# Gate rows by transfers in a two-half inference step, and another order of work between its halves

## The chip, the cores and the metric

One core of one Trainium2 chip runs one layer of a diffusion backbone for 384 tokens. The metric is the device time of one execution in microseconds (us), the median of three. A tile is given as partitions x columns. The engines are TensorE (PE), VectorE (DVE), ScalarE (ACT), GpSimd (POOL) and SyncE (SP), which issues most transfers.

## The reference, cut to what matters

```python
D_MODEL = 2048; SEQ = 128; DEC_SEQ = 256; FFN_HIDDEN = 5632      # 128 context and 256 latent tokens
def rmsnorm(x, g=None):
    y = x * rsqrt(mean(x * x, -1) + 1e-6)
    return y if g is None else y * g
# per layer, with mod = silu(cond) @ w_mod + b_mod, six vectors of 2048 for each of two conditions
# (c_ctx for context tokens, c for latent tokens): shift_m, scale_m, gate_m, shift_f, scale_f, gate_f
u  = (rmsnorm(x, g0) * (1 + scale_m) + shift_m) @ w_in            # 2048 x 5120
y1 = mixers(u) @ w_out                                           # attention and a scan; 2048 x 2048
x  = x + gate_m * rmsnorm(y1, g1)
h  = rmsnorm(x, g2) * (1 + scale_f) + shift_f
y2 = (silu(h @ w_gate) * (h @ w_up)) @ w_ffn_out                 # 2048 x 11264, 5632 x 2048
x  = x + gate_f * rmsnorm(y2, g3)
```

The last line but one of each half is where a gate comes in: one value for each of the 2048 columns, the same for all tokens of a condition.

## The kernel before

**Numbers and stages.** The 384 tokens are three blocks `tb` of 128 rows: block 0 is context, blocks 1 and 2 are latent. All matmuls are fp32 made of three rounded ones: a weight tile is split into `whi` (ScalarE, L468) and `wlo`, the remainder (VectorE, L1232); activations are split into `h_hi` and `h_lo` in the same way; TensorE adds hi x hi, lo x hi and hi x lo. Weights come as tiles of 1 MB in a fixed order, `PLAN`. The stages are: modulation and input projection (40 steps), output projection (16 steps), the work between the halves, FFN up (44 pairs of tiles), FFN down (4 groups `n` of 512 columns with 11 tiles `q` each, counted `v = 11 n + q`).

**Weight slots.** `tile_slots` gives each tile one of six slots of raw weights, the one that comes free first. SyncE issues each tile's transfer as soon as the slot's previous tile was used (`w_used`). The split is at most one tile ahead of TensorE: `whi` has room for two tiles, and `wlo` is written over the raw tile.

**Order.** Each engine's instructions are written out by hand. `gap(s, tb)` is what an engine does after block tb of step s: attention pieces, adds of a partial y1 (L1498) and, in the last four steps of the output projection, the row sums of y1 (ScalarE L644). The loops over s place splits (`lo`, `hi`) and gaps around each other.

**Gates.** The gate values lie as columns, one per partition, in `modc`. To multiply rows by them, every partition needs the whole row. `diagonal` (VectorE L1533) writes four 128x128 diagonal matrices of gate values into `diag` or `diag_b`; `gains` (TensorE L1114) multiplies a matrix of ones by them, so that a PSUM bank holds 512 gate values in every partition. There are 16 such calls: 8 in the last four steps of the output projection, two in each, and 8 in FFN down, after tiles q = 4 and 8 of each n. `y1_gate` (VectorE L1548) multiplies y1 by a bank, `y_gate` (L1542) does so for y2; the last group's banks are first copied to `gate_sb` on ScalarE (L777).

**Between the halves.** For each block VectorE does `residual(tb)`: gate the last 512 columns of y1, then four times x = x + y1 * scale over 512 columns (L1621). ScalarE squares x (L744) into `dump`, two halves per block, and sums them; GpSimd adds the two sums and takes the power -0.5 (L1886 to L1889); `norm_diagonal` (VectorE L1630) makes a diagonal of it; TensorE multiplies x by this diagonal (`x_transpose`, L960), which scales and transposes at once; VectorE applies scale and shift into `xnT` (L1304, L1306), ScalarE rounds to `h_hi` (L517), VectorE takes the remainder `h_lo` (L1311). The FFN's first tiles go k by k (k is one of 16 groups of 128 input rows), with six matmuls each (L1166 through `up_k`) and the transposes of k + 5 behind them. While TensorE waits it runs filler matmuls of 128 columns (L1155): 26, 10 and 5 ahead of the three blocks.

**End.** After the last tile VectorE gates the last columns and writes x in halves of 1024 columns (L1704); SyncE stores each half (L451).

## Time and profile before

| | us |
|---|---|
| median of three runs | 1792.37 |
| lowest, highest | 1792.31, 1792.74 |
| the profiled execution | 1791.8 |
| its span in the trace | 1790.0 |
| TensorE busy in it | 1761.8 |
| VectorE busy | 945.6 |
| ScalarE busy | 660.1 |
| GpSimd busy | 127.1 |

The span runs from the first to the last recorded instruction. A busy time is the union of an engine's instructions. The "chain that ended last" is followed back from the last instruction, at each step to whatever released it. One fp32 matmul from unsplit operands shows as two records. Matmuls are pipelined, so that the distance between starts, and not a record's length, is what one costs.

### The profile page before, as it was taken

The page shows a single profiled execution, that of the slowest core. Times are in us where ns is not written, and L with a number is a line of the kernel's source. Part 1 is how long each engine was busy: PE and PEld are TensorE (multiplying, and loading weights), DVE is VectorE, ACT ScalarE, POOL GpSimd, SP SyncE. Part 2 cuts the span into 40 slices and gives each one's busy share as a digit, 9 for nine tenths or more (in the row PEclk, how much of TensorE's full clock was granted, in tenths as well). Part 3 has the DMA queues.
Part 4 walks back from the last instruction along what each step waited for, and adds up shares of the span by engine and source line. Part 5 has one row for each costly group of instructions (what it writes and reads, how often), then busy time and mean ns, then how long its engine had stood idle before and what let it go on. Part 6 is the DMA issues. An engine that isn't in the chain of part 4 may idle for free.

```text
span 1790.0 us, 22643 instructions
## 1 busy us (share of the span) xinstructions
PE 1761.8 (98%) x9491; PEld 1524.9 (85%) x9491; DVE 945.6 (53%) x1276; ACT 660.1 (37%) x952; POOL 127.1 (7%) x179
## 2 busy tenths in 40 slices
PE   6999999999999999999999999999999999999998
PEld 4676666677778879999999999999999988888886
DVE  5465578633557677355665633333333455555554
ACT  3432354434564343222222222222222344444542
POOL 1001145410300010000000000000000000000000
PEclk9999999999999999999999999999999999999999
DMA  9998777765422333345545533333333333333321
GB/s 397 368 335 311 288 293 288 285 241 234 141 95 90 116 148 118 129 177 188 196 180 191 204 123 131 128 119 140 118 123 136 118 135 124 119 140 118 124 112 71
DMA packets 47190, 317.37 MB, mean 177 GB/s; under 512 B 5449, under 2 KB 7681, under 8 KB 10289
## 3 DMA queue, kind: packets, MB, share of 16 engines
q1 hardware_dynamic: 44736, 305.35, 45.5%
q0 software_dynamic: 2288, 10.56, 1.8%
q8 instruction: 75, 1.23, 0.3%
q14 instruction: 27, 0.21, 0.0%
q10 hardware_dynamic: 64, 0.02, 0.0%
HBM read 310.52 MB, written 5.39 MB: 176 GB/s over the span
## 4 chain that ended last, share of the span: by engine, by line
PE 96%; DVE 1%; DMA 1%; ACT 1%; POOL 0%; issue 0%; SPq 0%; DVEq 0%; POOLq 0%
PE ps L1166 41%; PE ps L943 8%; PE ps L945 8%; PE ps L944 8%; PE ps L837 7%; PE ps L838 7%; PE ps L836 7%; PE ps L815 4%; PE ps L1056 1%; PE ps L1079 1%; PE ps L1114 1%; PE ps L903 1%; PE ps L905 1%; PE ps L904 1%; PE ps L1006 1%; DMA xT<-in_x_t 0%
## 5 line engine op out<-in xcount | busy, mean ns | idle before, releaser
L1232 DVE TENSOR_TENSOR wlo<-raw,whi 128x1024 fp32r<-128x1024 f32 x376 | 459.0, 1233 | 687.2 <-ACT whi L468 687.1
L468 ACT ACTIVATE whi<-raw 128x1024 fp32r<-128x1024 f32 x376 | 392.3, 1058 | 831.4 <-PE ps L1166 507.0
L1166 PE MATMUL ps<-h_hi,whi 128*128 128x384 f32 x1408 | 471.4, 335 | 0.5 <-DVE h_lo L1311 0.5
L1166 PE MATMUL ps<-h_hi,wlo 128*128 128x384 f32 x1408 | 470.4, 334 | 0.0
L1166 PE MATMUL ps<-h_lo,whi 128*128 128x384 f32 x1408 | 470.3, 334 | 0.0
L1166 PEld LDWEIGHTS ps<-h_hi,whi 128*128 128x128 f32 x1408 | 264.3, 188 | 0.7 <-issue 0.7
L1166 PEld LDWEIGHTS ps<-h_lo,whi 128*128 128x128 f32 x1408 | 264.3, 188 | 0.0
L1166 PEld LDWEIGHTS ps<-h_hi,wlo 128*128 128x128 f32 x1408 | 264.3, 188 | 0.0
L943 PE MATMUL ps<-whi,h_hi 128*128 128x512 f32 x624 | 259.9, 417 | 0.0
L945 PE MATMUL ps<-wlo,h_hi 128*128 128x512 f32 x624 | 244.5, 392 | 0.0
L944 PE MATMUL ps<-whi,h_lo 128*128 128x512 f32 x624 | 243.6, 390 | 0.0
L836 PE MATMUL ps<-whi,j_hi 128*128 128x512 f32 x516 | 204.0, 395 | 0.0
L838 PE MATMUL ps<-wlo,j_hi 128*128 128x512 f32 x516 | 200.9, 389 | 0.0
L837 PE MATMUL ps<-whi,j_lo 128*128 128x512 f32 x516 | 200.9, 389 | 0.0
L943 PEld LDWEIGHTS ps<-whi,h_hi 128*128 128x128 f32 x624 | 117.2, 188 | 54.3 <-issue 30.3
L945 PEld LDWEIGHTS ps<-wlo,h_hi 128*128 128x128 f32 x624 | 117.1, 188 | 26.0
L944 PEld LDWEIGHTS ps<-whi,h_lo 128*128 128x128 f32 x624 | 117.5, 188 | 25.1 <-issue 1.9
L836 PEld LDWEIGHTS ps<-whi,j_hi 128*128 128x128 f32 x516 | 96.9, 188 | 21.8 <-issue 1.9
L837 PEld LDWEIGHTS ps<-whi,j_lo 128*128 128x128 f32 x516 | 96.8, 188 | 21.8 <-issue 1.9
L838 PEld LDWEIGHTS ps<-wlo,j_hi 128*128 128x128 f32 x516 | 96.8, 188 | 20.2
L1647 DVE TENSOR_TENSOR j_lo<-h3T,j_hi 128x1536 fp32r<-128x1536 f32 x44 | 77.4, 1758 | 8.4 <-ACT j_hi L771 8.4
L1869 POOL TENSOR_TENSOR smalls<-smalls 128x3 f32<-128x3 f32 x2 | 0.4, 190 | 1027.0 <-ACT ps L734 998.2
(257 smaller groups left out, 1362.1 us busy)
## 6 DMA issues: line engine op xcount, KB each, us to landing
raw<-in_weights SPq DMA_DIRECT2D x277, 1024.0 KB, 4.8
raw_x<-in_weights SPq DMA_DIRECT2D x6, 1024.0 KB, 19.5
xT<-in_x_t SPq DMA_DIRECT2D x4, 768.0 KB, 6.8
out<-x_sb SPq DMA_DIRECT2D x6, 512.0 KB, 2.7
x_sb<-in_x_sample POOLq DMA_DIRECT2D x1, 2048.0 KB, 12.2
sbc<-silu_rows POOLq DMA_DIRECT2D x1, 2048.0 KB, 8.1
raw<-in_weights SPq DMA_DIRECT2D x2, 512.0 KB, 18.4
gw<-in_lru_gate_w SPq DMA_DIRECT2D x4, 256.0 KB, 2.8
```

What stands on the lines that cost most here:

```text
L468: nc.scalar.activation(whi[:, 2 * (g % RING) + b], raw_of(t)[:, HK * b:HK * b + HK].rearrange("p k n -> p (k n)"), ACT.Copy).then_inc(w_hi, 1)
L815: ins = nc.tensor.matmul(ps[mod_bank(m)][32 * kk:32 * kk + 32, :], stat[:, 2 * k:2 * k + 32], raw_of(t)[:, kk, :], start=(kg == 0), stop=( ...
L836: nc.tensor.matmul(acc, xh[:, kk + HK * b, xs], wh[:, cols], start=(k == 0), stop=False)
L837: nc.tensor.matmul(acc, xl[:, kk + HK * b, xs], wh[:, cols], start=False, stop=False)
L838: ins = nc.tensor.matmul(acc, xh[:, kk + HK * b, xs], wl[:, cols], start=False, stop=(k == k_last))
L903: nc.tensor.matmul(acc, h_hi[:, k, xs], wh[:, cols], start=(k == 0), stop=False)
L943: nc.tensor.matmul(acc, h_hi[:, k, xs], wh[:, cols], start=begin, stop=False)
L944: nc.tensor.matmul(acc, h_lo[:, k, xs], wh[:, cols], start=False, stop=False)
L945: ins = nc.tensor.matmul(acc, h_hi[:, k, xs], wl[:, cols], start=False, stop=end)
L1166: return nc.tensor.matmul(ps[bank][:, 0:T], w[:, k % KH * P:(k % KH + 1) * P], xs[:, k, :], start=first, stop=last)
L1232: V.tensor_tensor(wlo[:, 2 * SLOT[t] + b], raw_of(t)[:, HK * b:HK * b + HK].rearrange("p k n -> p (k n)"), whi[:, 2 * (g % RING) + b].bitc ...
L1647: V.tensor_tensor(j_lo[v % 2][:, :, :], h3T[:, KG * q:KG * q + KG, :], j_hi[v % 2][:, :, :].bitcast(F32), ALU.subtract).then_inc(jl, 1)
```

## The change

**Gate rows.** `diagonal` and `gains` go, with all their calls, and `diag_b` and `gate_sb`. Gate columns are transposed instead: for each condition one matmul against the identity turns 16 columns of `modc` into a [16 x 128] tile; ScalarE copies both to `rows_g`; GpSimd stores them to DRAM (`gate_rows`) and reads them back with partition step 0, so that all 128 partitions hold the row of 2048. For the first gate this goes to `gate_r`, four pieces of 1024 columns laid over parts of `h_hi` and `h_lo` that the output projection has used up; the transposes stand at the end of the input projection, and the transfers wait for 12 adds of y1. For the second it goes to `gate2`, laid over weight slots 4 and 5. So tiles of FFN down may use four slots only. Its transposes stand behind down tile v = 1, the copy behind v = 3.

**Order between the halves.** In the last steps the gates of y1 stand ahead of the split of the next tile. After the last step the last add comes first, then the three residuals, then the diagonals. Block 2 is squared in four parts. Filler is 45, 0 and 2. For the first FFN tiles the four matmuls on `h_hi` stand ahead of the two on `h_lo`, each with a wait of its own.

**End.** The last block is stored in three parts: 1024, 512 and 512 columns.

The diff, cut to its core:

```diff
-        open_to = range(RAW + EXTRA) if key in early else range(RAW)
+        open_to = range(RAW + EXTRA) if key in early else range(RAW - 2 if key[0] == "down" else RAW)
...
+    gate_r = [[at(f"gate_r{c}{b}", [P, D // 2], H0 + off) for b, off in enumerate(offs)]
+              for c, offs in enumerate(((30720, 43008), (6144, 18432)))]
+    rows_g = at("rows_g", [KD, 2, P], P0 + 3072)
-    gate_sb = at("gate_sb", [P, 2, NC], U0 + 8192)
-    diag_b = at("diag_b", [P, KG, P], U0 + 43008)
+    gate2 = [at(f"gate2_{c}", [P, D], RW0 + (RAW - 2 + c) * KG * NC * 4) for c in range(2)]
...
+        def y_parts(tb):
+            ends = [0, D // 2, D] if tb < TB - 1 else [0, D // 2, D - NC, D]
+            return [slice(a, b) for a, b in zip(ends, ends[1:])]
+        def x1_parts(tb):
+            return 4 if tb == TB - 1 else 2
...
@@ ScalarE
                 if g == TB * IN_STEPS - 1:
                     act.wait_ge(st_t, 1)
+                    nc.scalar.activation(rows_g[:, :, :].rearrange("k c p -> k (c p)"), ps[3][0:KD, P:3 * P], ACT.Copy).then_inc(st_cp, 1)
...
-                for b in range(2):
+                w = D // x1_parts(tb)
+                for b in range(x1_parts(tb)):
                     act.wait_ge(x1_ok, 2 * tb + b + 1)
...
+                    if v == 3:
+                        act.wait_ge(gf_tr, 1)
+                        nc.scalar.activation(rows_g[:, :, :].rearrange("k c p -> k (c p)"), ps[7][0:KD, 0:2 * P], ACT.Copy).then_inc(gf_row, 1)
...
-            for j in range(2):
-                nc.scalar.activation(gate_sb[:, j, :], ps[7 - j][:, :], ACT.Copy).then_inc(gate_ok, 1)
@@ TensorE
-                nc.tensor.matmul(ps[gain_bank(idx)][:, :], ones[:, :], src[:, :, :].rearrange("p f n -> p (f n)"),
-                                 start=True, stop=True).then_inc(g_ps, 1)
...
+                    pe.wait_ge(gm_ok, 1)
+                    nc.tensor.transpose(ps[3][0:8, 0:P], stc[:, :], ident[:, :])
+                    for c in range(2):
+                        ins = nc.tensor.transpose(ps[3][0:KD, P + c * P:2 * P + c * P], modc[:, G_M:G_M + KD, c], ident[:, :])
...
-                if g >= TB * (STEPS - OUT_N) and g % TB < 2:
-                    gains(2 * (g // TB - STEPS + OUT_N) + g % TB)
...
-            for tb, busy in enumerate((26, 10, 5)):
+            for tb, busy in enumerate((45, 0, 2)):
...
+                pe.wait_ge(h_hs, KD + k + 1)
+                for part in range(2):
+                    b, wh, wl = now[part]
+                    up(k, part, wh, h_hi, k == 0, False)
+                    up(k, part, wl, h_hi, False, False)
                 pe.wait_ge(h_ls, KD + k + 1)
                 for part in range(2):
                     b, wh, wl = now[part]
-                    ins = up_k(k, part, wh, wl)
+                    ins = up(k, part, wh, h_lo, False, k == KD - 1)
...
-                    if q in (4, 8):
-                        gains(8 + 2 * n + q // 4 - 1)
+                    if v == 1:
+                        pe.wait_ge(gf_ok, 1)
+                        for c in range(2):
+                            ins = nc.tensor.transpose(ps[7][0:KD, c * P:P + c * P], modc[:, G_F:G_F + KD, c], ident[:, :])
@@ VectorE
-                                    ps[7 if tb == 0 else 6][:, :], ALU.mult).then_inc(y_g, 1)
+                                    gate2[1 if tb == 0 else 0][:, n * NC:(n + 1) * NC], ALU.mult).then_inc(y_g, 1)
...
-                if s:
-                    lo(*step_key(s + 1))
                 if n > 0:
                     for tb in range(TB):
                         y1_gate(n - 1, tb)
+                if s:
+                    lo(*step_key(s + 1))
...
+            gap(STEPS - 1, 2)
             residual(0)
-            gap(STEPS - 1, 2)
             residual(1)
+            residual(2)
             norm_diagonal(0)
-            residual(2)
             norm_diagonal(1)
@@ GpSimd
+            pool.dma_start(gate_d.rearrange("c (k p) -> k c p", p=P), rows_g[:, :, :]).then_inc(grow_w, 16)
...
+            pool.wait_ge(grow_w, 16)
+            pool.wait_ge(y_add, TB * OUT_N)
+            for c in range(2):
+                for b in range(2):
+                    pool.dma_start(gate_r[c][b][:, :], bass.AP(tensor=gate_d.tensor, offset=D * c + D // 2 * b,
+                                                               ap=[[0, P], [1, D // 2]])).then_inc(grow_in, 16)
...
+            pool.wait_ge(gf_row, 1)
+            pool.dma_start(gate2_d.rearrange("c (k p) -> k c p", p=P), rows_g[:, :, :]).then_inc(gf_w, 16)
+            pool.wait_ge(gf_w, 16)
+            pool.wait_ge(w_used, used(*LAST_UP))
+            for c in range(2):
+                pool.dma_start(gate2[c][:, :], bass.AP(tensor=gate2_d.tensor, offset=D * c, ap=[[0, P], [1, D]])).then_inc(gf_in, 16)
```

How it moves instructions, at two places. VectorE from the last adds of the output projection to the diagonals, before (`y_3` is y1's last group of 512 columns, `smalls` holds row scales):

```order
L1498 TENSOR_TENSOR y_3_120<-y_3_120,ps 128x512 [waits y_add,acc_ps] x2
L1548 TENSOR_TENSOR y_3_120<-y_3_120,ps 128x512 [waits y_sq,g_ps,x1_in]
L1621 SCALAR_TENSOR_TENSOR x_sb<-y_0_117,smalls,x_sb 128x512 [waits rs_done,y_g]
...
L1498 TENSOR_TENSOR y_3_120<-y_3_120,ps 128x512 [waits y_add,w_used]
L1548 TENSOR_TENSOR y_3_120<-y_3_120,ps 128x512 [waits y_sq,g_ps]
...
L1630 TENSOR_SCALAR diag<-par,smalls 128x128 [waits g_ps,rs_done]
L1548 TENSOR_TENSOR y_3_120<-y_3_120,ps 128x512 [waits y_sq,g_ps]
...
L1630 TENSOR_SCALAR diag<-par,smalls 128x128 [waits rs_done]
L1232 TENSOR_TENSOR wlo<-raw_86,whi 128x1024 [waits w_hi]
```

The same place in the changed kernel:

```order
L1507 TENSOR_TENSOR y_3_130<-y_3_130,ps 128x512 [waits y_add,acc_ps] x2
L1507 TENSOR_TENSOR y_3_130<-y_3_130,ps 128x512 [waits y_add,w_used,x1_in]
L1549 TENSOR_TENSOR y_3_130<-y_3_130,gate_r_114 128x512 [waits y_sq]
L1620 SCALAR_TENSOR_TENSOR x_sb<-y_0_127,smalls,x_sb 128x512 [waits rs_done,y_g]
...
L1549 TENSOR_TENSOR y_3_130<-y_3_130,gate_r_112 128x512 [waits y_sq]
...
L1549 TENSOR_TENSOR y_3_130<-y_3_130,gate_r_112 128x512 [waits y_sq]
...
L1629 TENSOR_SCALAR diag<-par,smalls 128x128 [waits grow_w,rs_done]
L1629 TENSOR_SCALAR diag<-par,smalls 128x128 [waits rs_done]
L1241 TENSOR_TENSOR wlo<-raw_86,whi 128x1024 [waits w_hi]
```

The last add moved ahead of the first gate and residual, and the first diagonal behind the third residual; the gates read `gate_r` and no PSUM bank.

TensorE after the output projection, before:

```order
L1155 MATMUL ps<-par,ones 128x128 x25
L960 MATMUL ps<-diag,x_sb 128x128 [waits xn_done,x1_ok,y_g]
...
L1155 MATMUL ps<-par,ones 128x128 x10
...
L1155 MATMUL ps<-par,ones 128x128 x5
L960 MATMUL ps<-diag,x_sb 128x128 [waits xn_done,x1_ok,y_g]
L960 MATMUL ps<-diag,x_sb 128x128 x8
L1166 MATMUL ps<-h_hi,whi 128x384 [waits h_ls,w_lo]
L1166 MATMUL ps<-h_lo,whi 128x384
```

In the changed kernel:

```order
L1156 MATMUL ps<-par,ones 128x128 x44
L977 MATMUL ps<-diag,x_sb 128x128 [waits xn_done,x1_ok,y_g]
...
L1156 MATMUL ps<-par,ones 128x128 x2
L977 MATMUL ps<-diag,x_sb 128x128 [waits xn_done,x1_ok,y_g]
L977 MATMUL ps<-diag,x_sb 128x128 x8
L1167 MATMUL ps<-h_hi,whi 128x384 [waits h_hs,w_lo]
L1167 MATMUL ps<-h_hi,wlo 128x384
L1167 MATMUL ps<-h_hi,whi 128x384
L1167 MATMUL ps<-h_hi,wlo 128x384
L1167 MATMUL ps<-h_lo,whi 128x384 [waits h_ls]
```

The filler moved ahead of block 0's transposes, and the first matmuls wait for `h_hs`, which counts columns of `h_hi`, and no longer for `h_ls`, which counts those of `h_lo`.

## Rows read from the trace of the kernel before

**Rows 1.** The page, chain that ended last: share of the span by engine.
```profile
PE 96%; DVE 1%; DMA 1%; ACT 1%; POOL 0%; issue 0%; SPq 0%; DVEq 0%; POOLq 0%
```

**Rows 2.** Chain in order of time: start us, us, engine, output, line, records.
```profile
494.82 0.48 PE ps L1096 x3
...
622.36 0.86 PE ps L1114 x2
...
632.33 0.86 PE ps L1114 x2
...
677.15 1.06 PE ps L1166 x6
...
678.88 1.06 PE ps L1166 x6
...
1672.74 0.86 PE ps L1114 x2
...
1730.77 0.86 PE ps L1114 x2
...
1764.32 0.86 PE ps L1114 x2
```

**Rows 3.** Lines L1498 and L1548: count, ns min/median/max, first and last start us.
```profile
L1498 DVE TENSOR_TENSOR y1p<-y1p,ps x3: 686/687/687, 571.4 to 578.1; 128x512 f32<-128x512 f32 x3
...
L1548 DVE TENSOR_TENSOR y<-y,ps x12: 678/680/686, 634.4 to 666.3; 128x512 f32<-128x512 f32 x12
```

**Rows 4.** Timeline between the halves: start, us, engine, line, operation, [idle before <-releaser].
```profile
659.37 5.96 PE L1155 MATMUL ps<-par,ones 128*128 128x128 f32 x52
...
661.30 0.68 DVE L1498 TENSOR_TENSOR y<-y,ps 128x512 f32<-128x512 f32 x1
661.90 0.68 DVE L1548 TENSOR_TENSOR y<-y,ps 128x512 f32<-128x512 f32 x1
...
662.61 2.74 DVE L1621 SCALAR_TENSOR_TENSOR x_sb<-y,smalls,x_sb 128x512 f32<-128x512 f32 x4
...
669.66 1.44 POOL L1886 TENSOR_SCALAR smalls<-smalls 128x1 f32<-128x1 f32 x1 [0.87 <-ACT dump L744]
669.75 1.06 ACT L744 ACTIVATE dump<-x_sb 128x1024 f32<-128x1024 f32 x1 [0.17 <-DVE x_sb L1621]
669.83 1.22 DVE L1232 TENSOR_TENSOR wlo<-raw,whi 128x1024 fp32r<-128x1024 f32 x1
...
671.18 0.19 POOL L1888 TENSOR_TENSOR smalls<-smalls 128x1 f32<-128x1 f32 x1
671.45 0.55 POOL L1889 TENSOR_TENSOR smalls<-smalls 128x1 f32<-128x1 f32 x1
672.03 0.29 DVE L1630 TENSOR_SCALAR diag<-par,smalls 128x128 f32<-128x128 f32 x1 [0.98 <-POOL smalls L1889]
672.47 2.25 PE L960 MATMUL ps<-diag,x_sb 128*128 128x128 f32 x18 [0.38 <-DVE diag L1630]
...
673.86 0.52 ACT L517 ACTIVATE h_hi<-xnT 128x384 fp32r<-128x384 f32 x1 [2.01 <-DVE xnT L1306]
...
675.21 0.41 PE L1166 MATMUL ps<-h_hi,whi 128*128 128x384 f32 x1 [0.49 <-DVE h_lo L1311]
```

**Rows 5.** Transfer issues: tile, queue, count, KB each, us to landing.
```profile
sbc<-silu_rows POOLq DMA_DIRECT2D x1, 2048.0 KB, 8.1
```

**Rows 6.** Weight tiles issued in FFN down, 1416 to 1776 us.
```profile
DMA to landing us min/median/max: 4.7/4.8/6.2
```

**Rows 7.** Weight tiles issued from 690 to 780 us, among them one beside `sbc`.
```profile
DMA to landing us min/median/max: 4.7/4.9/11.1
```

**Rows 8.** Windows: us, busy PE, PEld, DVE, ACT, POOL, granted clock, DMA share, GB/s.
```profile
665.40:666.50 1.10, 0.01 (x1) 0.04 (x1) 0.44 (x2) 1.10 (x3) 0.83 (x3) 1.00 0.00 0
675.20:694.50 19.30, 19.29 (x134) 19.30 (x135) 17.47 (x41) 6.81 (x13) 0.00 (x0) 1.00 0.00 1
```

**Rows 9.** The same for the last transfers.
```profile
1787.00:1789.00 2.00, 0.00 (x0) 0.00 (x0) 0.00 (x0) 0.00 (x0) 0.00 (x0) 0.50 1.00 406
```

More of the change, by code:

```diff
@@ L447, in _ @@
             for tb in range(TB):
[L448 to L449 removed]
+                for b, part in enumerate(y_parts(tb)):
                     sp.wait_ge(fin, 2 * tb + b + 1)
                     sp.dma_start(y_p[0, :, part] if tb == 0 else y_s[0, (tb - 1) * P:tb * P, part], x_sb[:, tb, part]).then_inc(out_st, 16)
[L452 removed]
+            sp.wait_ge(out_st, (2 * TB + 1) * 16)
         @block.scalar
@@ L741, in _ @@
                     hi("up", 0, 1, bs=(0,))
-                for b in range(2):
+                w = D // x1_parts(tb)
+                for b in range(x1_parts(tb)):
                     act.wait_ge(x1_ok, 2 * tb + b + 1)
-                    nc.scalar.activation(dump[:, 2 * tb + b, :], x_sb[:, tb, D // 2 * b:D // 2 * (b + 1)], ACT.Square,
+                    nc.scalar.activation(dump[2 * tb + b * w // (D // 2)][:, b * w % (D // 2):b * w % (D // 2) + w],
+                                         x_sb[:, tb, w * b:w * (b + 1)], ACT.Square,
                                          scale=D ** -0.5, accum_out=xsh[:, 2 * tb + b:2 * tb + b + 1]).then_inc(sq_done, 1)
@@ L1097, in turn_back @@
                 ins.then_inc(cv_ps, 1)
-            def gain_bank(idx):
-                return (4 + 2 * (idx // 2 % 2) + idx % 2) if idx < 8 else 7 - idx % 2
-            def gains(idx):
-                pe.wait_ge(dg_ok, idx + 1)
-                n = idx // 2
-                if idx < 4:
-                    pe.wait_ge(ex, NU)
-                    pe.wait_ge(o_ev, NU)
-                elif idx < 8:
-                    pe.wait_ge(y_g, 3 * (n - 1))
-                else:
-                    pe.wait_ge(y_g, 3 * n)
-                src = diag_b if idx < 8 and idx % 2 else diag
-                nc.tensor.matmul(ps[gain_bank(idx)][:, :], ones[:, :], src[:, :, :].rearrange("p f n -> p (f n)"),
-                                 start=True, stop=True).then_inc(g_ps, 1)
             def gap(g):
@@ L1523, in gap, with y_gate @@
                     V.tensor_tensor(h_lo[:, k, :], ps[3][:, 0:T], h_hi[:, k, :].bitcast(F32), ALU.subtract).then_inc(cv_lo, 1)
-            def diagonal(g0, n, cond, idx):
-                if idx >= 8:
-                    dve.wait_ge(g_ps, idx)
-                elif idx >= 2:
-                    dve.wait_ge(g_ps, idx - 1)
-                dst = diag_b if idx < 8 and idx % 2 else diag
-                for f in range(4):
-                    ins = V.tensor_scalar(dst[:, f, :], ident[:, :], modc[:, g0 + 4 * n + f, cond:cond + 1], None, ALU.mult)
-                ins.then_inc(dg_ok, 1)
-            def y_gate(y, n, idx):
-                dve.wait_ge(g_ps, idx + 2)
+            def y_gate(y, n):
+                if n == 0:
+                    dve.wait_ge(gf_in, 32)
                 for tb in range(TB):
@@ L1556, in _ @@
                     gap(s - 1, 2)
-                if n >= 0:
-                    diagonal(G_M, n, 0, 2 * n + 1)
                 if s in (2, 3):
@@ L1604, in _ @@
                     dve.wait_ge(mod_col, len(MOD_K0))
+                    gain(SC_F, 2, True)
+                if s == IN_STEPS - 3:
                     gain(G_M, 1, False)
-                    gain(SC_F, 2, True)
+                    dve.sem_inc(gm_ok, 1)
                 if s >= EARLY * KG:
                     gap(s, 1)
-                if -1 <= n < OUT_N - 1:
-                    diagonal(G_M, n + 1, 1, 2 * n + 2)
             dve.wait_ge(x1_in, 32)
@@ L1691, in _ @@
                     if q == 1 and n:
-                        y_gate(y2, n - 1, 8 + 2 * (n - 1))
-                    if q in (3, 6):
-                        diagonal(G_F, n, 1 if q == 3 else 0, 8 + 2 * n + (q == 6))
-            dve.wait_ge(gate_ok, 2)
+                        y_gate(y2, n - 1)
             dve.wait_ge(y_g, 21)
@@ L1698, in _ @@
                 dve.wait_ge(y_sq, 12 + tb + 1)
-                V.tensor_tensor(y2[:, tb, 3 * NC:], ps[3 + tb][:, :], gate_sb[:, 0 if tb == 0 else 1, :], ALU.mult).then_inc(y_g, 1)
+                V.tensor_tensor(y2[:, tb, 3 * NC:], ps[3 + tb][:, :], gate2[1 if tb == 0 else 0][:, 3 * NC:], ALU.mult).then_inc(y_g, 1)
                 dve.wait_ge(y_g, 21 + tb + 1)
                 dve.wait_ge(rs_done, 8 + tb)
-                for b in range(2):
-                    c = slice(D // 2 * b, D // 2 * (b + 1))
+                for c in y_parts(tb):
                     V.scalar_tensor_tensor(x_sb[:, tb, c], y2[:, tb, c], yrs[:, tb:tb + 1], x_sb[:, tb, c],
@@ L1886, in _ @@
                 link(G.tensor_scalar(r, xsh[:, 2 * tb:2 * tb + 1], 1.0, EPS, ALU.mult, ALU.add))
-                pool.wait_ge(sq_done, 4 + 2 * tb + 2)
-                link(G.tensor_tensor(r, r, xsh[:, 2 * tb + 1:2 * tb + 2], ALU.add))
+                for b in range(1, x1_parts(tb)):
+                    pool.wait_ge(sq_done, 4 + 2 * tb + b + 1)
+                    link(G.tensor_tensor(r, r, xsh[:, 2 * tb + b:2 * tb + b + 1], ALU.add))
                 G.tensor_tensor(r, r, negh[:, 0:1], ALU.pow).then_inc(rs_done, 1)
```

36 lines of the change are left out of this document (21 added, 15 removed).

## Prediction

> **What bounds the kernel now.** I read the page first: the chain that ended last is TensorE for 96% of its length [rows 1]. Where TensorE runs without a break, an instruction taken from it is time taken from the kernel. Two stretches differ. Between the halves (659.4 to 675.2 us) TensorE has ended the output projection and waits for VectorE, ScalarE and GpSimd to turn y1 into the first columns of the FFN's input; its matmuls of L1155 there are filler [rows 4]. After 1782 us only VectorE and the output transfers are left [rows 9]. So I read the gain rows in the chain in order of time, then the timeline between the halves, then landings and the tail.
>
> **Gain matmuls on TensorE.** Each of the 16 calls of `gains` puts one fp32 matmul of 512 columns (two records) between tiles of the running stream. Its price I take from distances between them in the chain [rows 2]: in the down projection 1672.74 to 1730.77 is 7 tiles and one gain, 58.03 us, and 1730.77 to 1764.32 is 4 tiles and one gain, 33.55. The difference, 24.48, is 3 tiles, so a tile is 8.16 and a gain 33.55 - 32.64 = 0.91 us. In the output projection 622.36 and 632.33 lie 9.97 apart, one tile and two gains: (9.97 - 8.16) / 2 = 0.905. The chain gives the two records alone 0.86, the lower bound. All 16 go: 16 x 0.905 = **14.5 us** (13.8 to 14.6). The four steps that shrink from 9.97 to 8.16 keep their cover: VectorE has in one of them three adds (0.68), three gates (0.68) and two splits of half a tile (1.22) [rows 4], 6.5 us, and its 8 small multiplies for diagonals leave. Nothing else was late there, since the chain shows TensorE alone.
>
> **Transposes added.** Two pairs, one at the end of the input projection, one after the second tile of the down projection. Three transposes of L1096 take 0.48 together in the chain [rows 2]. If a pair costs what those three do, the four cost 1.0 us; at a third of it each, with the common start-up left out, 0.5. I take **+0.5**, since they stand in a stream that hides the start-up. ScalarE's two small copies of 256 columns are not in the chain's way: no matmul waits for their buffers within a tile.
>
> **The rows' transfers.** The first gate's four transfers (2 MB together) are issued by GpSimd once twelve adds of y1 are done, 578.1 plus 0.7 [rows 3]; a broadcast of the same size (`sbc`) landed in 8.1 us [rows 5]. They are in by 590, the first gate is at 634.4 [rows 3]: 44 us of cover. On GpSimd they stand ahead of the load of x_sb, which waits for twelve adds more anyway. The second gate: the gain at 1672.74 stands behind 31 tiles and 5 gains of down, so down begins at 1672.74 - 31 x 8.16 - 5 x 0.91 = 1415; transposes near 1432, copy near 1448, one small store and two broadcasts of 1 MB, three landings of at most 8.1, so in by 1473; first used in tile 12, 1513. Cost 0. A weight tile that met the broadcast of `sbc` came in after 11.1 us [rows 7], which bounds what the next part must stand.
>
> **Four slots for down tiles, not six.** A slot is freed at the end of the tile four before, so its transfer is issued 3 tiles (24.5 us) before TensorE wants the tile, and 2.3 of them go to the split (1.06 on ScalarE, 1.22 on VectorE [rows 4]). A landing up to 22 us stalls nothing; in this stage it was 4.8, at most 6.2 [rows 6]. Cost 0, and one tile late by 2 us at the worst.
>
> **Between the halves**, in the times of the profile before [rows 4]. VectorE took the last add at 661.30, since the residual of block 0 stood ahead. Now the add goes first, near 659.57 (the filler starts at 659.37 while the last matmul drains), 0.60 to the next start. Three times a gate (0.71) and a residual of four (2.74, of which 0.08 overlaps the next instruction) follow: 659.57 + 0.60 + 3 x 3.37 = 670.28, where the third residual ended near 669.7 before; no diagonal is waited for in between. The two diagonals (0.19 each) and the split (1.22) end at 671.9. ScalarE: block 1's last square starts when residual 1 is done, 667.1, and takes 1.06; the conversion of L468 as long; then four squares of 512 columns for block 2 in place of two of 1024, 0.63 each (half of 1.06 and 0.1 of start), read out by 671.9, where the last was done near 670.9 (669.75 + 1.06 and the read). GpSimd adds one part per square. Its one-column operation at 669.66 took 1.44 us, to 671.10, beside VectorE's split that ended at 671.05, where an add takes 0.19 at 671.18 and leads to the next in 0.27 [rows 4]: so I let it come free at 671.9, then two adds of 0.27 and the power of 0.55 end at 673.0. The last diagonal comes at 673.0 instead of 672.03: **1.0 later**.
>
> The Trainium skill says why (GPSIMD Engine Reference, Specifications): GpSimd shares its SBUF interfaces with VectorE and contends with instructions that have two SBUF inputs. That rule speaks against the change, whose gates now read their second operand from SBUF and not PSUM; by it alone all of GpSimd's steps here would be long ones, and the sum would be rival B's.
>
> TensorE: 45 fillers at 0.229 (26 in 5.96) end at 669.7, before the first diagonal, so they delay nothing; the blocks' transposes follow, those of block 2 at 673.0 + 0.44, 18 records at 0.115, to 675.5. (The diagonal at 672.03 led to records at 672.47.) Before, the first up matmul waited for h_lo until 675.21, and the second k began at 677.15. Now the four matmuls that need h_hi alone go first (ready at 673.86 + 0.52 + 1.0 = 675.4 [rows 4]), so the first k takes 1.73 like the others (678.88 - 677.15 [rows 2]) and the second begins at 675.5 + 1.73 = 677.25: **+0.1**. The split order gives back 0.9 of the 1.0. From both sides: 0.9 shorter if the diagonal isn't late, 1.1 longer if GpSimd loses one more long operation.
>
> **The tail.** The last gate's copies on ScalarE go; they lay under matmuls. The last block's output leaves in parts of 512, 256 and 256 KB. But the 16 DMA engines are full from 1787 to 1789, at 406 GB/s [rows 9]: bytes bound the end, not the last part's size. **0** (0.3 shorter to 0.2 longer).
>
> **Sum**: -14.5 + 0.5 + 0.1 + 0 = -13.9. The profiled execution took 1791.8 (span 1790.0 and 1.8 around it), so 1777.9; the median of three runs is 0.57 higher, 1792.37, so **1778.5 us**. With all bounds: 14.6 - 0.5 + 0.9 + 0.3 = 15.3 off, 1777.1; and 13.8 - 1.1 - 1.1 - 0.2 - 2 = 9.4 off, 1783.
>
> **Rivals.** A, a shorter middle: VectorE's early add starts the whole row of work 1.7 us sooner, and if GpSimd keeps up, the last diagonal is not late; with a smaller last transfer 1777.0 or less. For it: VectorE's wait for the first diagonal goes. Against: four squares cost 2.5 us of ScalarE where two cost 2.1 [rows 4], behind the conversion.
> B, GpSimd is starved: VectorE now works without a pause from 659.6 to 671.9, all three row sums fall beside it. If its last four steps take 0.8 each (half-way between 0.19 and 1.44 [rows 4]) and not 0.2 to 0.55, the diagonal comes 2 us later still: 1780.5.
> C, the stream is no longer TensorE's alone: late weight tiles or late gate rows. Half of the down stage's 7.2 us lost, 3.6, and one stall at a broadcast of up to its added landing, 11.1 - 4.9 = 6.2 [rows 7]: 1782 to 1788. Against it: the landings [rows 6, 7]. That the change doesn't do what it says would look the same: rows that land after 634.4 or 1513 hold VectorE, then the banks, then TensorE.
> D, slower than before: the clock. TensorE's granted clock stayed at 1.00 through a pause of 1.10 between the halves, so at 2.4 GHz [rows 8]; at the end of the kernel 0.50 is granted [rows 9], 1.2 GHz. Filler now stands in one block of 45, with 0 and 2 after it. If the clock fell in the pause after 669.7, and stayed down over the first k loop (19.3 us at full clock [rows 8]), that loop would take 38.6: 1778.5 + 19.3 = 1797.8. It decides at three quarters of the loop: 13.9 us lost. Against it: the pauses I find (1.0 before block 0's transposes, 0.9 before block 2's) are no longer in all than the old ones (1.10, 0.38 and 0.49 among them [rows 4, 8]).
> The Trainium skill (TensorE: Matmul & The Clock Gate, Why this matters for your kernels) says that a long idle gap between bursts returns the clock to its low level; the trace shows none at pauses of this size.
>
> **How the numbers follow.** Forecast (1777.1 to 1780) 0.70; A 0.10; B (1780 to 1782) 0.11; C 0.06; D 0.03. The range 1776.5 to 1781.5 holds the first, nearly all of A and most of B, some 0.85. A measurement of this kernel tells 0.2% (3.6 us) from no change. Faster by more than that needs under 1788.8: all of the forecast, A and B and most of C, 0.95; same 0.02; slower 0.03.
>
> **What the new profile would show.** No group of 128x512 matmuls from `ones` and `diag`; tiles of down 8.16 us apart without a break of 0.91; four transfers of gate rows landed before 600; SP's waits before down tiles as long as a tile; the last diagonal some 13.6 us after the filler's start (12.7 before) and matmuls on h_hi ahead of h_lo; granted clock 1.00 through. Wrong would be: idle time of TensorE before down tiles, a GpSimd row over 1.5 us between the halves, or a wait of VectorE for gate rows.

## The result

Both kernels ran on the same chip, in turns.

| | before | changed |
|---|---|---|
| median, us | 1792.34 | 1779.06 |
| lowest, highest | 1791.71, 1792.74 | 1778.71, 1779.31 |
| span of the profiled execution | 1790.0 | 1777.3 |

The changed kernel is faster: ratio 0.9927, 95% interval 0.9915 to 0.994. The prediction was 1778.5, range 1776.5 to 1781.5.

**Profile after.** The chain that ended last, share of the span by engine, answers [rows 1]:

```profile
PE 97%; DVE 1%; DMA 1%; issue 0%; ACT 0%; POOL 0%; SPq 0%; DVEq 0%; POOLq 0%
```

TensorE still sets the time. The chain in order of time (start us, us, engine, output, line, records), changed kernel, answers [rows 2]. No pair from `ones` and `diag` is left in it:

```profile
610.72 0.67 PE ps L1096 x6
...
666.85 2.25 PE ps L977 x18
669.09 1.12 PE ps L1167 x6
670.21 0.67 PE ps L977 x6
670.88 1.06 PE ps L1167 x6
...
688.18 720.75 PE ps L1167 x4158
1765.58 0.70 ACT ysd L797 x2
```

Three rows of the same view of the kernel before that were not shown yet, for the same points of the program:

```profile
610.39 0.67 PE ps L1079 x6
...
694.46 720.75 PE ps L1166 x4158
...
1778.86 0.70 ACT ysd L780 x2
```

The row of 720.75 us is TensorE's unbroken run of up matmuls from the last transpose on. The row of `ysd` is the last one in the chain; in both kernels one more such square starts 2.7 us behind it and is not in the chain. With the filler's start (659.37 in [rows 4], 652.44 in the timeline below) these rows cut the span into stretches:

| stretch | before | after | difference |
|---|---|---|---|
| start to the last attention matmul (610.39, 610.72) | 610.39 | 610.72 | +0.33 |
| from there to the filler: output projection | 48.98 | 41.72 | -7.26 |
| filler to the second k (677.15, 670.88) | 17.78 | 18.44 | +0.66 |
| second k to the start of the row of 720.75 | 17.31 | 17.30 | -0.01 |
| from there to the chain's last `ysd`: FFN up and down | 1084.40 | 1077.40 | -7.00 |
| last `ysd` to the end of the span | 11.14 | 11.72 | +0.58 |
| sum | 1790.0 | 1777.3 | -12.70 |

Two stretches hold the gain, 14.26 together. Three others give 1.57 back. Windows of both kernels show TensorE busy for all of the output projection's end (48.30 of 48.30 us before, 611.00 to 659.30; 41.40 of 41.40 after, 611.00 to 652.40). So the 7.26 are work taken from TensorE there, and not a wait that went.

Timeline between the halves, changed kernel (start, us, engine, line, operation, [idle before <-releaser]); it answers [rows 4]:

```profile
652.44 10.21 PE L1156 MATMUL ps<-par,ones 128*128 128x128 f32 x90
652.69 0.69 DVE L1507 TENSOR_TENSOR y<-y,ps 128x512 f32<-128x512 f32 x1 [2.09 <-PE ps L962]
653.30 0.68 DVE L1549 TENSOR_TENSOR y<-y,gate_r 128x512 f32<-128x512 f32 x1
...
663.66 1.44 POOL L1892 TENSOR_TENSOR smalls<-smalls 128x1 f32<-128x1 f32 x1
663.84 1.21 DVE L1241 TENSOR_TENSOR wlo<-raw,whi 128x1024 fp32r<-128x1024 f32 x1
...
664.01 0.61 ACT L761 ACTIVATE dump<-x_sb 128x512 f32<-128x512 f32 x1
...
665.57 0.19 POOL L1892 TENSOR_TENSOR smalls<-smalls 128x1 f32<-128x1 f32 x1 [0.19 <-POOL smalls L1892]
665.83 0.54 POOL L1893 TENSOR_TENSOR smalls<-smalls 128x1 f32<-128x1 f32 x1
666.41 0.29 DVE L1629 TENSOR_SCALAR diag<-par,smalls 128x128 f32<-128x128 f32 x1 [1.35 <-POOL smalls L1893]
...
668.91 0.41 PE L1167 MATMUL ps<-h_hi,whi 128*128 128x384 f32 x1
...
670.64 0.42 PE L1167 MATMUL ps<-h_hi,whi 128*128 128x384 f32 x1
```

The last of these rows is the first matmul of the second k. The timeline of the kernel before has it here:

```profile
676.91 0.42 PE L1166 MATMUL ps<-h_hi,whi 128*128 128x384 f32 x1
```

The last diagonal stands 13.97 us behind the filler's start, where it was 12.66. VectorE was idle for 2.09 us ahead of the last add: it waits for the last matmul, and the first gate and residual now wait with it. The row at 668.91 shows the other side: TensorE's first matmul on `h_hi` starts at 668.91 and waits for nothing, 2.50 us behind the diagonal, where [rows 4] have 675.21 - 672.03 = 3.18 and a wait for h_lo.

Transfers, from the page of the changed kernel (tile, queue, count, KB each, us to landing), and the store's line in the page of before:

```profile
out<-x_sb SPq DMA_DIRECT2D x5, 512.0 KB, 2.7
gate_r<-gate_rows POOLq DMA_DIRECT2D x4, 512.0 KB, 7.6
gate<-gate_rows POOLq DMA_DIRECT2D x2, 1024.0 KB, 7.3
```

```profile
out<-x_sb SPq DMA_DIRECT2D x6, 512.0 KB, 2.7
```

The same two tiles by line in the changed kernel (count, ns min/median/max, first and last start):

```profile
L1549 DVE TENSOR_TENSOR y<-y,gate_r x12: 680/684/686, 628.8 to 660.1; 128x512 f32<-128x512 f32 x12
L1859 POOL DMA_DIRECT2D gate_r<-gate_rows x4: 530/542/613, 579.7 to 581.4; - x4
```

```profile
L1540 DVE TENSOR_TENSOR y<-y,gate x9: 684/684/686, 1503.2 to 1683.9; 128x512 f32<-128x512 f32 x9
...
L1904 POOL DMA_DIRECT2D gate<-gate_rows x2: 539/555/571, 1430.5 to 1431.0; - x2
```

With the longest landings, 8.9 and 9.4 us, the rows lie in SBUF some 38 and 63 us before their first use.

Weight tiles issued in FFN down of the changed kernel, which answers [rows 6], and what SyncE waited for there (us in total, times, longest):

```profile
DMA to landing us min/median/max: 4.6/4.8/8.3
```

```profile
SPq L462 <- PE ps L855: 305.1, 39, 8.1
```

SyncE waits as long as a tile before each transfer, so the slots are used as soon as they come free. TensorE has no idle time. Windows of the changed kernel (us, busy PE, PEld, DVE, ACT, POOL, clock, DMA share, GB/s) answer [rows 8]:

```profile
662.65:663.87 1.22, 0.00 (x0) 0.03 (x1) 1.22 (x5) 1.22 (x5) 0.81 (x2) 1.00 0.00 0
665.90:666.85 0.95, 0.01 (x1) 0.04 (x1) 0.29 (x1) 0.00 (x0) 0.48 (x1) 1.00 0.03 9
668.90:688.20 19.30, 19.30 (x136) 19.30 (x135) 18.07 (x42) 7.35 (x14) 0.00 (x0) 1.00 0.00 1
...
1430.00:1765.00 335.00, 335.00 (x1480) 277.39 (x1479) 174.84 (x131) 149.91 (x149) 2.50 (x7) 1.00 0.35 126
```

The granted clock is full in both pauses and in the first k loop.

### The profile page after: what moved, and what is told of

Read it like the earlier page. It is cut to its first block, busy times and chain, and to the rows that moved or that the text cites. A ratio compares the mean times of both kernels' runs of the same rounds, so it can differ in the third digit from the quotient of the medians.

```text
span 1777.3 us, 22538 instructions
## 1 busy us (share of the span) xinstructions
PE 1749.4 (98%) x9475; PEld 1521.1 (86%) x9475; DVE 932.9 (52%) x1213; ACT 660.5 (37%) x956; POOL 133.4 (8%) x189
## 4 chain that ended last, share of the span: by engine, by line
PE 97%; DVE 1%; DMA 1%; issue 0%; ACT 0%; POOL 0%; SPq 0%; DVEq 0%; POOLq 0%
PE ps L1167 41%; PE ps L960 8%; PE ps L962 8%; PE ps L961 8%; PE ps L855 7%; PE ps L854 7%; PE ps L853 7%; PE ps L832 4%; PE ps L1073 1%; PE ps L1096 1%; PE ps L920 1%; PE ps L922 1%; PE ps L921 1%; PE ps L1023 1%; PE ps L977 1%; DMA xT<-in_x_t 1%
## 5 line engine op out<-in xcount | busy, mean ns | idle before, releaser
L832 PE MATMUL ps<-raw,stat 128*32 128x512 f32 x552 | 66.3, 598 | 0.0
```

Of the source, the lines that this page charges most:

```text
L832: ins = nc.tensor.matmul(ps[mod_bank(m)][32 * kk:32 * kk + 32, :], stat[:, 2 * k:2 * k + 32], raw_of(t)[:, kk, :], start=(kg == 0), stop=( ...
```

## Experiments

All times are medians. "Last diagonal" and "second k" are distances from the filler's start, so that what happened earlier in the kernel, which moved that start by up to 1.2 us between kernels that are alike up to there, does not enter. The kernel before has 12.66 and 17.78 there, the changed one 13.97 and 18.44.

### What one gain costs TensorE

Kernel before; in FFN down each of the 8 gain matmuls is done twice.

```diff
-                nc.tensor.matmul(ps[gain_bank(idx)][:, :], ones[:, :], src[:, :, :].rearrange("p f n -> p (f n)"),
-                                 start=True, stop=True).then_inc(g_ps, 1)
+                for _ in range(2 if idx >= 8 else 1):
+                    ins = nc.tensor.matmul(ps[gain_bank(idx)][:, :], ones[:, :], src[:, :, :].rearrange("p f n -> p (f n)"),
+                                           start=True, stop=True)
+                ins.then_inc(g_ps, 1)
```

> The kernel before with the matmul of each of the eight gains in FFN down issued twice; all else is left. Theory: a gain costs its full issue time in the stream of matmuls, 0.86 to 0.905 us each, nothing of it is covered: the span rises by 6.9 to 7.2, from 1790.0 to about 1797.1, the median to 1799.4. Rival: part of the 13 us that the change gained came from elsewhere (VectorE's diagonals gone, the waits of TensorE for them), and a second matmul behind the first costs less, under 5 us.

Measured: 1799.22 us, ratio 1.0039 (1.0025 to 1.0052), span 1796.7. From the start of the row of 720.75 to the last `ysd` it took 1091.29 us, 6.89 more than before, 0.86 for each added matmul. That is the length of the two records in [rows 2], the prediction's lower bound. The one that goes is worth 0.905 to 0.91 in both stages: 7.26 / 8 = 0.91, and (7.00 + 0.24) / 8 = 0.905 with the 0.24 of the two transposes, read from the changed kernel's timeline under "Transposes" further down. So a gain's price was the full matmul and some 0.04 of a seam with the stream. This shows the main term from the opposite side: the stream has no slack that would swallow or soften it.

### Slots: four, three and two

Kernel before; FFN down gets fewer weight slots, all else stays. Two runs have 3 and 4 in place of the 2:

```diff
-        open_to = range(RAW + EXTRA) if key in early else range(RAW)
+        open_to = range(RAW + EXTRA) if key in early else range(RAW - 2 if key[0] == "down" else RAW)
```

> The kernel before with four weight slots in place of six for the tiles of FFN down and nothing else. Theory: a landing of up to 22 us is covered and 4.8 is measured, so 0: span 1790.0 within the 0.6 us by which executions of one stretch differ. Rival: the shallower ring costs something in each group that the removed matmuls hid in the changed kernel: 1 us or more.

Measured: 1792.10 us, ratio 1.0 (0.999 to 1.001); the row of 720.75 to the last `ysd` 1084.40 us, to the hundredth the old value. Four slots cost nothing.

> The kernel before with three slots of raw weights for the tiles of FFN down in place of six; nothing else is changed. A slot is freed two tiles (16.3 us) before its next tile is wanted. By the prediction's sum (7.1 us needed) and by the rival's (10.5) alike it costs nothing: 1792 us, within 0.1% of the kernel before. Were it slower by 5 us or more, the four slots of the changed kernel, with 24.5 us, would stand nearer to their limit than either sum says.

Measured: 1792.41 us, ratio 1.0 (0.9991 to 1.001). Three slots cost nothing either, as both sums had it, so this run does not tell them apart.

> The kernel before with two slots of raw weights for the tiles of FFN down in place of six; nothing else is changed. It measures how much cover the split of a tile really needs, since the prediction counted only 2.3 us for it behind the landing. A slot is then freed one tile (8.16 us) before TensorE wants its next tile. By the prediction's sum a landing of 4.8 and the 2.3 of the split, 7.1, fit into 8.16: cost 0, 1792 us. The rival sum takes the whole row of work behind the landing: on ScalarE the two halves of whi (1.06 and 1.04) and what stands in its order beside them, then VectorE's wlo halves (1.22 each) before TensorE goes on, 4.8 + some 5.4 + 0.3 for the issue = 10.5, more than 8.16: some 2.3 us of idle TensorE before each of some 42 tiles of down, 97 us, so some 1890 us. The two are told apart by TensorE's idle time before the tiles of down.

Measured: 1835.14 us, ratio 1.024 (1.0224 to 1.0255), 43.2 us more between those two points, 1.03 a tile over some 42. The kernel with two slots, timeline in FFN down:

```profile
1601.47 0.33 SPq L446 DMA_DIRECT2D raw<-in_weights  x1
...
1606.18 2.01 ACT L468 ACTIVATE whi<-raw 128x1024 fp32r<-128x1024 f32 x2 [5.20 <-DMA raw<-in_weights]
1607.27 2.36 DVE L1232 TENSOR_TENSOR wlo<-raw,whi 128x1024 fp32r<-128x1024 f32 x2 [4.50 <-ACT whi L468]
1608.09 1.47 ACT L771 ACTIVATE j_hi<-h3T 128x1536 fp32r<-128x1536 f32 x1
1609.60 1.76 DVE L1647 TENSOR_TENSOR j_lo<-h3T,j_hi 128x1536 fp32r<-128x1536 f32 x1
...
1611.41 0.19 PEld L836 LDWEIGHTS ps<-whi,j_hi 128*128 128x128 f32 x1 [0.56 <-DVE j_lo L1647]
```

From the issue at 1601.47 to TensorE's start at 1611.41 pass 9.94 us: 4.7 of transfer, 2.01 for both halves of `whi`, then the activations of that step, `j_hi` and `j_lo`, which stand behind the split on the same two engines. The prediction's 4.8 + 2.3 = 7.1 would have fitted into 8.16, and is refuted. The rival's 10.5 was near, but its 97 us were not: if TensorE idles before one tile, the next slot's transfer has that idle time as cover too. A tile starts 9.94 behind the end of the tile two before it, so two tiles take 9.94 + 8.16 = 18.10 us, 0.89 a tile more than 8.16, some 37 us for 42; 43.2 came out. TensorE's waits for `j_lo` in that stage add up to 27.3 us in 29 places, so not every tile waits as this sum has it, and what makes up the rest was not found. By the same 5.2, an estimate, TensorE stands with four slots a landing of up to 24.5 - 5.2 = 19.3 us, not 22. Nothing of that was needed: the longest landing was 8.3.

### The order of VectorE

Changed kernel, but VectorE has the old order (residual 0 ahead of the last add, a diagonal between the residuals), and the filler is 26, 10 and 5 again.

```diff
-            for tb, busy in enumerate((45, 0, 2)):
+            for tb, busy in enumerate((26, 10, 5)):
...
-            gap(STEPS - 1, 2)
             residual(0)
+            gap(STEPS - 1, 2)
             residual(1)
-            residual(2)
             norm_diagonal(0)
+            residual(2)
             norm_diagonal(1)
```

> The changed kernel with VectorE's old order between the halves (residual 0, last add, residual 1, diagonal 0, residual 2, diagonal 1, split, diagonal 2) and the old filler of 26, 10 and 5; block 2 still squared in four parts, h_hi still first. Theory: in the changed kernel the last diagonal came 14.0 us after the filler's start and before the change 12.7, since GpSimd's additions for block 2 fall beside VectorE's split; the old order brings it back to about 12.8, so the span falls by 1.2 from 1777.3 to 1776.1. Rival: the new order is worth its 1.7 us earlier add and something else held the last diagonal; the span stays at 1777.3 or rises to about 1778.

Measured: 1778.36 us, ratio 0.9922 (0.9907 to 0.9937); last diagonal 13.17, second k 17.63. The diagonal was expected near 12.8 and comes 0.4 later: here too one add of GpSimd is long beside VectorE's split, 1.14 us from 663.73. The second k comes 0.8 us sooner than with the new order. The medians lie 0.7 apart, which their intervals don't tell apart; the distances within the kernel do. The filler, changed along with the order, does not set the last diagonal: the changed kernel's 45 end at 662.65, and TensorE then waits 1.22 us for a diagonal; and from the last diagonal to its transposes it is 0.44 us in both. So the new order of VectorE costs 0.8 us here, and the other changes of this part outweigh the rest: with the old order the place is 0.15 quicker than before.

### Squares in two parts

Changed kernel; block 2 is squared in two halves like the others.

```diff
-            return 4 if tb == TB - 1 else 2
+            return 2
...
-                    if n % 2 or tb == TB - 1:
+                    if n % 2:
```

> The changed kernel with block 2 squared in two parts of 1024 columns, so that GpSimd has one addition for it and not three. Theory: GpSimd is what is late; ScalarE ends 0.2 later, but two additions of 0.27 go, so the last diagonal comes 0.4 earlier and the span falls from 1777.3 to 1776.9. Rival: ScalarE's last square sets the diagonal, and the span rises by 0.3 to 1777.6.

Measured: 1778.86 us, ratio 0.9925 (0.991 to 0.994); last diagonal 13.33, second k 17.77. The four parts cost 0.64 us of the last diagonal's 1.31, half of it, and 0.67 at the second k. With two, GpSimd's last steps are these:

```profile
664.44 1.21 DVE L1241 TENSOR_TENSOR wlo<-raw,whi 128x1024 fp32r<-128x1024 f32 x1
...
665.45 0.25 POOL L1892 TENSOR_TENSOR smalls<-smalls 128x1 f32<-128x1 f32 x1 [1.08 <-ACT dump L761]
665.78 0.54 POOL L1893 TENSOR_TENSOR smalls<-smalls 128x1 f32<-128x1 f32 x1
666.36 0.29 DVE L1629 TENSOR_SCALAR diag<-par,smalls 128x128 f32<-128x128 f32 x1 [0.70 <-POOL smalls L1893]
```

GpSimd waits 1.08 us for ScalarE and has one short add left. With four parts it has three, the first of them the long one at 663.66 beside VectorE's split, in the changed kernel's timeline above.

### One wait before the first up matmuls

Changed kernel; the six matmuls of each k wait for `h_lo` together, in the old order.

```diff
-                pe.wait_ge(h_hs, KD + k + 1)
-                for part in range(2):
-                    b, wh, wl = now[part]
-                    up(k, part, wh, h_hi, k == 0, False)
-                    up(k, part, wl, h_hi, False, False)
                 pe.wait_ge(h_ls, KD + k + 1)
                 for part in range(2):
                     b, wh, wl = now[part]
-                    ins = up(k, part, wh, h_lo, False, k == KD - 1)
+                    ins = up_k(k, part, wh, wl)
```

> The changed kernel with the six matmuls of each k of the first FFN tiles in the old order behind one wait for h_lo. Theory: only the first k is touched. From the last diagonal to the second k it took 5.1 us before the change and 4.5 after; so the span rises by 0.6 from 1777.3 to 1777.9. Rival: the transposes of block 2 hold TensorE anyway, and the span stays at 1777.3.

Measured: 1779.94 us, ratio 0.9931 (0.9916 to 0.9946); last diagonal 13.97, second k 19.12. So `h_hi` first is worth 0.68 at the second k. It is the one of the three edits of this part that pays.

### The last store in two parts

Changed kernel; the last block is stored as 1024 and 1024 columns.

```diff
-            ends = [0, D // 2, D] if tb < TB - 1 else [0, D // 2, D - NC, D]
+            ends = [0, D // 2, D]
...
-            sp.wait_ge(out_st, (2 * TB + 1) * 16)
+            sp.wait_ge(out_st, 2 * TB * 16)
```

> The changed kernel with the last block stored in two parts of 512 KB again and not three. Theory: the stretch from the last square (ScalarE, ysd) to the end was 11.1 us before the change and 11.7 after; 0.13 of it is VectorE's third instruction, the rest the two parts with rows of 2 KB. The span falls by 0.6 from 1777.3 to 1776.7. Rival: the longer stretch comes from the gate read out of weight slots, and the span stays.

Measured: 1779.15 us, ratio 0.9926 (0.991 to 0.9943); the chain's last `ysd` to the end 11.05 us in place of 11.72. The filler of its profiled execution starts 0.6 us later than in the changed kernel's, which hides the 0.67 in the span, and the medians don't resolve it; within the kernel it is plain. VectorE's last residual in the timeline of the changed kernel, and in that of this one:

```profile
1771.01 2.61 DVE L1700 SCALAR_TENSOR_TENSOR x_sb<-y,smalls,x_sb 128x1024 f32<-128x1024 f32 x3
```

```profile
1771.58 2.48 DVE L1700 SCALAR_TENSOR_TENSOR x_sb<-y,smalls,x_sb 128x1024 f32<-128x1024 f32 x2
```

The stores of the changed kernel, by its transfer issues in the last 13 us:

```profile
out<-x_sb SPq DMA_DIRECT2D x2, 256.0 KB, 3.2
```

The residual takes 0.13 longer in three instructions, and parts of half the size land in 3.2 us, where this kernel's six of 512 KB take 2.7 like those of before.

### The changed kernel again

> The changed kernel itself, beside the others on one chip. Theory: span 1777.3 within 0.6, median 1779; filler's start to the second k of the FFN 18.5 us, last square to the end 11.7. A rival reading, that the middle and the end vary from run to run as much as the edits moved them, would show 0.5 us or more of difference in these two stretches.

Measured: 1779.03 us, ratio 0.9927 (0.9912 to 0.9943), span 1776.9; filler at 651.95, last diagonal 13.96, second k 18.43, the row of 720.75 to the last `ysd` 1077.41. The distances up to the last `ysd` come back within 0.02, the one from there to the end within 0.1 (11.8 for 11.7). The filler's start moved, by 0.5. So the rival reading, differences of 0.5 in these two stretches from run to run, is refuted.

### Gates ahead of the last add

If VectorE's idle 2.09 us ahead of the last add are the place, the first two gates fit there, since they need `gate_r` and old sums alone. This kernel does that, moves half of ScalarE's conversion for FFN tile 1 ahead of the last row sum, squares in two parts, stores in two parts, and has filler 38, 0 and 2.

```diff
+            hi("up", 0, 1, bs=(0,))
...
-                if tb == TB - 1:
-                    hi("up", 0, 1, bs=(0,))
...
-            for tb, busy in enumerate((45, 0, 2)):
+            for tb, busy in enumerate((38, 0, 2)):
...
-                y1_gate(3, tb)
+                if tb == TB - 1:
+                    y1_gate(3, tb)
...
+            y1_gate(3, 0)
+            y1_gate(3, 1)
```

> The changed kernel with VectorE's gates of y1's last columns for blocks 0 and 1 ahead of the last add, in the 2.1 us in which it waited; ScalarE's conversion for the second FFN tile ahead of the last square of y1; two squares for block 2; filler 38, 0, 2; and the last block stored in two parts. Theory: VectorE's row of work ends 1.3 us sooner, ScalarE's squares of block 2 no longer stand behind a conversion, GpSimd has two additions less: the last diagonal 12.0 us after the filler's start (14.0 in the changed kernel), second k at 16.5 (18.5); with 0.7 from the end the span falls from 1777.3 to 1774.6, the median to 1776.4. Rival: GpSimd, beside a VectorE that never pauses, gives all of it back, the last diagonal stays near 13.4 as with two squares alone, and the span is 1776.

Measured: 1776.48 us, ratio 0.9914 (0.9898 to 0.993), span 1774.6; last diagonal 11.80, second k 16.26, the chain's last `ysd` to the end 11.04. It is 2.6 us faster than the changed kernel by the medians; 2.2 lie between the halves and 0.7 at the end, by the distances. Of the 2.2 the squares are 0.7, as the run above showed; the other 1.5 belong to the gates and the conversion together (the filler was shortened with them), and were not told apart. It also shows what a gate from SBUF does to GpSimd. Its timeline:

```profile
650.88 1.36 DVE L1548 TENSOR_TENSOR y<-y,gate_r 128x512 f32<-128x512 f32 x2
650.92 0.70 POOL L1881 TENSOR_TENSOR smalls<-smalls 128x1 f32<-128x1 f32 x1 [2.58 <-ACT ysq L659]
...
651.70 0.98 POOL L1882 TENSOR_TENSOR smalls<-smalls 128x1 f32<-128x1 f32 x1
```

And the same two steps of GpSimd in the kernel before, whose gate reads PSUM:

```profile
657.66 0.69 DVE L1548 TENSOR_TENSOR y<-y,ps 128x512 f32<-128x512 f32 x1 [0.29 <-ACT ysq L644]
657.68 0.19 POOL L1876 TENSOR_TENSOR smalls<-smalls 128x1 f32<-128x1 f32 x1 [5.81 <-ACT ysq L644]
657.95 0.58 POOL L1877 TENSOR_TENSOR smalls<-smalls 128x1 f32<-128x1 f32 x1
```

The one-column add takes 0.70 and not 0.19, the power 0.98 and not 0.58.

## Why the prediction was right, and where its terms were off

**The gain matmuls: 14.5, held.** With the transposes predicted at +0.5, the three stretches of TensorE's stream should give -14.0; they gave -7.26, -7.00 and +0.33, together -13.93 (the last holds some 0.1 of what varies between executions). The price from distances of tiles (0.905) was the right one, and the added matmuls bound it from below at 0.86. No cover was missing: TensorE doesn't idle in FFN down, and the output projection shrank by all of its eight gains.

**Transposes: +0.5, held.** The pair in FFN down, in the timeline of the changed kernel:

```profile
1424.90 0.39 PE L855 MATMUL ps<-wlo,j_hi 128*128 128x512 f32 x1
1425.13 0.38 PE L1219 MATMUL ps<-par,modc 128*16 128x128 f32 x2
1425.27 0.48 PE L853 MATMUL ps<-whi,j_hi 128*128 128x512 f32 x1
1425.59 0.39 PE L854 MATMUL ps<-whi,j_lo 128*128 128x512 f32 x1
```

Neighbours stand 0.227 apart there without it (8.16 us for the 36 of a tile), so the pair costs 0.69 - 0.45 = 0.24. That is the 0.24 by which the stretch shrank less than 8 x 0.905. The first pair costs 0.21, by the same view: from the small transpose ahead of it to the second matmul of the stream behind it are 0.56 us (486.74 to 487.30), and 0.35 (486.64 to 486.99) before. Together 0.45. The size was right, but the step shows no row for it: a third of 0.48 is 0.16 for each, 0.64 for four, and the rest of the way to 0.5 is a guess. The remainder of the +0.33 ahead of the output projection is no effect of the change: the same program had 610.72 and 610.22 there in two executions.

**Rows' transfers and slots: 0, held, with a wrong sum behind it.** The rows land within 9.4 us and wait for their use; one weight landing reached 8.3. That four slots suffice was shown alone. But the step "2.3 of them go to the split" counted half of `whi` and half of `wlo`, and left out that `j_hi` and `j_lo` stand behind the split on the same engines: 5.2 us, as the kernel with two slots showed. At four slots this changes nothing, so the 0 came out right in spite of the sum. By the same sum two slots would have been called free, and they cost 43 us.

**Between the halves: +0.1 predicted, +0.66 measured.** Two terms were mis-sized. "The last diagonal comes at 673.0, 1.0 later": it comes 1.31 later. GpSimd's long operation ended at 663.66 + 1.44 = 665.10, 12.66 behind the filler's start, where the step has 12.53, and ahead of its last add it sat idle for 0.19, which the step does not have. The other term is "the split order gives back 0.9": it gave 0.65 (from the diagonal to the second k 5.12 before, 4.47 now), and 0.68 when tested alone. The first up matmul comes 2.50 behind the diagonal, for 3.18 before, just as the step says, and "so the first k takes 1.73 like the others" held: 670.64 - 668.91 = 1.73 in the timeline. What failed is the comparison. The step added 1.73 to a time of the timeline, 675.5, and held the sum against 677.15, which is the second k of the chain's view. The chain puts that k 0.24 behind its first matmul in the timeline: 677.15 for 676.91 before, 670.88 for 670.64 now. Within the timeline it is 4.88 before and 4.23 now, which gives the same 0.65, and 4.23 is what the step has (677.25 - 673.0 = 4.25). The diagonal's 0.3 and these 0.24 are the 0.56 by which the place was missed. By the runs the edits here are: VectorE's order +0.7 with squares in two parts and +0.8 with four, the squares +0.5 in the old order and +0.7 in the new, `h_hi` first -0.68 (the first +0.7 and the +0.5 stand against 17.78 - 0.68 = 17.10 for a kernel that was not run).

**The tail: 0 predicted, +0.58 measured.** The step that failed is "bytes bound the end, not the last part's size". The full DMA engines of [rows 9] carry a part that VectorE has just finished, and each landing starts behind VectorE: 2.48 became 2.61, and 2.7 became 3.2 to 3.3. The kernel with two parts gave it back (11.05). Why the smaller part lands later stays open.

**Rivals.** A (1777.0): no. The early add was there, but gate and residual of block 0, which started 1.7 and 0.7 us ahead of the filler before, now wait behind it, and VectorE is idle for 2.09 first. B (1780.5) was right in kind and too large: GpSimd's long steps are there (0.71, 0.87, 1.44), but most lie where nobody waits for them, and only the 1.44 counts. The Trainium skill (GPSIMD Engine Reference, Specifications) names contention with VectorE instructions that have two SBUF inputs; the trace agrees, 0.70 beside a gate with both operands in SBUF against 0.19 beside one that reads PSUM. C and D did not come: no idle TensorE in FFN down, and the granted clock at 1.00, its level of 2.4 GHz, behind pauses of 1.22 and 0.95.

The forecast missed the median by 0.56 us. Against the profiled spans it missed by 1.2: -12.7 for -13.9, nearly all of it the 0.56 of the middle and the 0.58 of the tail. The medians show less of this miss because the profiled execution of before, from which the sum starts, stood 0.57 under its median, and that of the changed kernel (1777.3 and the same 1.8 around it) did not. So half of the closeness to the median is luck: it hangs on which executions were profiled.

## What to carry to other kernels

Where one engine runs alone, price an instruction by the distance between neighbours with and without it; that held to 0.1 us over 16 of them. Take both ends of such a distance from the same view: the chain and the timeline put the same matmuls 0.24 us apart, a third of what the order of six matmuls was worth. A buffer's cover must be held against the whole row of work behind the landing, the next step's operations on the same engines too. And an operation that has become free of its producer (here the gate rows) is worth most in the idle time ahead of a wait: two gates moved there, with one conversion on ScalarE, gave 1.5 us, where the reordering of the work behind the wait cost 0.7 to 0.8.

## What the runs showed of the hardware

A store of 256 KB in rows of 2 KB landed in 3.2 us where one of 512 KB in rows of 4 KB took 2.7, on the same queue at the same place. The Trainium skill (DMA: Bandwidth & Descriptors, Specifications) gives 512 bytes as the least size for line rate. Both kinds of row are longer than that, so the figure does not tell them apart, and no run here tells whether the row length or the transfer just ahead of it is the cause.

A one-column operation of GpSimd that takes some 0.2 us took 1.44 when it began just ahead of VectorE's split (by 0.17), and it ended just behind the split each time: at 671.10 for 671.05 in [rows 4], at 665.10 for 665.05 in the changed kernel, at 664.87 for 664.82 with VectorE's old order, at 665.70 for 665.65 with two squares, where it began late and took 0.25. The add of 0.70 beside a gate from SBUF ends 0.05 behind that gate in the same way. The rows read as if such an operation is held until VectorE's instruction is over, so that its cost depends on where the two meet. They do not show it for every pair, and GpSimd's spans are rough in this profile: in the changed kernel an add at 658.09 took its 0.19 and the power at 658.36 took 0.87, to 659.23, while the residual's four instructions, with two inputs from SBUF as well, ran from 657.40 to 660.15.

A matmul from fp32 operands of 512 columns cost 0.86 us as an added neighbour of its like, and 0.905 as a guest in the stream (the distance between its neighbours with and without it).

Broadcasts from DRAM to 128 partitions landed in 6.3 to 8.9 us at 512 KB, four in flight, in 5.2 to 9.4 at 1 MB, two in flight, and in 8.1 at 2 MB in one transfer [rows 5].
